# Sharing out the sum jobs of a gated decoder layer on one core, with the first scaling of u and the splitting of the next block's features moved

## What is computed

```python
h = rmsnorm(x, norm_mix_g)
z = gelu(h @ a_w_in)                        # 1024 -> 2048
u, v = split(z, 2)
v = rmsnorm(v, a_v_g)
ws = tril(a_w_s)                            # 8 groups of 128 x 128
s = einsum('gts,bnsgc->bntgc', ws, v) + a_b_s
x = x + (u * s) @ a_w_out
a = relu(rmsnorm(x, norm_mlp_g) @ mlp_w1)
x = x + (a * a) @ mlp_w2
out = rmsnorm(x, final_g)
```

## Time and profile before

| | |
|---|---|
| median of 3 runs | 1854.7 us |
| lowest, highest | 1849.44, 1864.49 us |
| the profiled execution | 1849.99 us |
| its span, first to last instruction | 1847.7 us |
| mean granted TensorE clock | 0.984 of full speed |
| PE busy | 1784.2 us (97%) |
| DVE busy | 1138.0 us (62%) |
| ACT busy | 786.1 us (43%) |
| POOL busy | 445.4 us (24%) |

### The profile page before, as it was taken

One profiled execution on the slowest core, in us unless ns is written; L12 is line 12 of the kernel. 1 busy time (PEld: TensorE's weight loads), 2 busy tenths in 40 slices (PEclk: granted clock), 3 DMA queues, 4 the chain that ended last, 5 costly groups with the idle time before them and its releaser, 6 DMA issues.

```text
span 1847.7 us, 20069 instructions
## 1 busy us (share of the span) xinstructions
PE 1784.2 (97%) x8036; PEld 1481.4 (80%) x8036; DVE 1138.0 (62%) x1136; ACT 786.1 (43%) x862; POOL 445.4 (24%) x418
## 2 busy tenths in 40 slices
PE   9999299999899999999999999999999999999998
PEld 8788188888688888888878888888888888888886
DVE  3561487456288665665576665676567666866665
ACT  5822325462423744443463434454433335333333
POOL 2443542443442123330001311110234101000002
PEclk9999599999999999999999999999999999999999
DMA  9556375765566788886867777699977645854552
GB/s 362 218 190 231 136 272 205 274 250 183 205 228 248 292 271 269 279 288 216 302 234 252 255 256 250 222 401 319 309 281 279 248 182 188 299 196 182 187 206 108
DMA packets 135452, 451.68 MB, mean 244 GB/s; under 512 B 8128, under 2 KB 9152, under 8 KB 119616
## 3 DMA queue, kind: packets, MB, share of 16 engines
q1 hardware_dynamic: 101344, 323.77, 49.5%
q0 software_dynamic: 27344, 101.19, 15.3%
q10 hardware_dynamic: 6672, 25.44, 3.7%
HBM read 320.35 MB, written 130.02 MB: 244 GB/s over the span
## 4 chain that ended last, share of the span: by engine, by line
PE 79%; DMA 10%; POOL 6%; ACT 3%; issue 2%; DVE 1%; ACTq 0%; DVEq 0%; POOLq 0%
PE bank L1448 64%; PE bank L1409 8%; PE bank L1260 4%; DMA job<-in_mlp_w 2%; DMA job<-xs 2%; DMA w1sum<-job 1%; PE bank L1249 1%; DMA job<-in_a_w_out 1%; DMA w_raw<-in_a_w_in 1%; ACT junk L653 1%; DMA wosum<-job 1%; DMA xs<-job 1%; POOL x_rstd L495 1%; PE bank L1282 1%; POOL job L529 1%
## 5 line engine op out<-in xcount | busy, mean ns | idle before, releaser
L1448 PE MATMUL bank<-x_hi,u_hi 128*128 128x512 f32 x896 | 349.1, 390 | 1.2 <-DVE c L1158 1.2
L1448 PE MATMUL bank<-x_hi,u_lo 128*128 128x512 f32 x896 | 348.6, 389 | 0.0
L1448 PE MATMUL bank<-x_lo,u_hi 128*128 128x512 f32 x896 | 348.6, 389 | 0.0
L1448 PE MATMUL bank<-d_lo,a_hi 128*128 128x512 f32 x896 | 348.5, 389 | 0.0
L1448 PE MATMUL bank<-d_hi,a_hi 128*128 128x512 f32 x896 | 348.5, 389 | 0.0
L1448 PE MATMUL bank<-d_hi,a_lo 128*128 128x512 f32 x896 | 348.5, 389 | 0.0
L1158 DVE TENSOR_TENSOR Y<-bank,Y 128x512 f32<-128x512 f32 x208 | 137.9, 685 | 179.1 <-PE bank L1448 178.7
L925 DVE TENSOR_TENSOR u_lo<-u_raw,u_hi 128x1024 fp32r<-128x1024 f32 x112 | 149.0, 1331 | 147.7 <-ACT u_hi L610 147.4
L615 ACT ACTIVATE d_hi<-d_raw 128x2048 fp32r<-128x2048 f32 x56 | 107.4, 1918 | 288.5 <-DMA d_raw<-w2sum 161.0
L919 DVE TENSOR_TENSOR w_lo<-w_raw,w_hi 128x2048 fp32r<-128x2048 f32 x45 | 108.2, 2411 | 150.3 <-ACT w_hi L605 150.3
L1448 PEld LDWEIGHTS bank<-x_hi,u_hi 128*128 128x128 f32 x896 | 168.2, 188 | 36.5 <-DVE u_lo L925 1.9
(11 more groups left out here) (125 smaller groups left out, 2791.9 us busy)
## 6 DMA issues: line engine op xcount, KB each, us to landing
a_raw<-a2s SPq DMA_DIRECT2D x56, 1024.0 KB, 7.8
a2s<-sums SPq DMA_DIRECT2D x32, 1280.0 KB, 8.1
job<-in_mlp_w POOLq DMA_DIRECT2D x32, 1024.0 KB, 7.0
u_raw<-w1sum SPq DMA_DIRECT2D x64, 512.0 KB, 4.7
d_raw<-w2sum SPq DMA_DIRECT2D x32, 1024.0 KB, 4.9
w_raw<-in_a_w_in SPq DMA_DIRECT2D x31, 1024.0 KB, 5.9
u_raw<-in_mlp_w SPq DMA_DIRECT2D x48, 512.0 KB, 5.3
d_raw<-in_mlp_w SPq DMA_DIRECT2D x24, 1024.0 KB, 5.3
```

Source lines behind the costliest of these rows:

```text
L1448: ins = pe.matmul(bank_of(g, j)[:, :], stationary[x_part][:, k, j * P:(j + 1) * P], moving[y_part][:, k, :], start=i in (0, 1, 3) and k == ...
```

## The change

Three edits. (1) POOL: the jobs of the four blocks are 1 and 2, 1 and 6, 1 and 2, 1 and 7 (before and behind the block's `rstd` of v) in place of 1 and 5, then 2 and 4 three times; 21 are done in the first stage in place of 24, and 19 in place of 15 in the groups u. (2) DVE: `scale_u(q, 0)` stands ahead of the remainder of weight w+8. (3) DVE: the remainders of the next block's features are made in two halves, the first behind weight w+9 (before the gates 2 and 3), the second behind gates 4 and 5; with it PE waits for four tiles before unit w and for the other four before unit w+1. The tiles and the number of instructions stay the same on every engine.

```diff
             for q in range(BLOCKS):
-                next_jobs(2 if q else 1)
+                next_jobs(1)
                 rstd(v_sq, v_squares(q), v_ms, v_ms_done, v_rstd, v_rstd_done, q)
...
-                next_jobs(4 if q else 5)
+                next_jobs((2, 6, 2, 7)[q])
...
             for u in range(UP):
                 pool.wait_ge(products, step_done(u * STEPS))
                 if not UP // PAIRS - 2 <= u <= UP // PAIRS:
-                    next_jobs(2 if u < 2 else 1)
+                    next_jobs(2 if u in (0, 1, 2, 3, 10, 12) else 1)
...
                 split_w(w + 7)
+                scale_u(q, 0)
                 split_w(w + 8)
-                scale_u(q, 0)
                 gates(q, 0)
                 split_w(w + 9)
                 if q % 2:
                     split_o(q // 2, 0)
+                else:
+                    split_h(q + 1, range(KU))
                 gates(q, 2)
-                if q % 2 == 0:
-                    split_h(q + 1, range(KD))
                 scale_u(q, 1)
                 gates(q, 4)
                 if q % 2 == 0:
+                    split_h(q + 1, range(KU, KD))
                     gates(q, 6)
...
                 if q:
-                    pe.wait_ge(hT_ready, q * KD + KD)
+                    pe.wait_ge(hT_ready, q * KD + KU)
...
                 token_major(hT[q], w, bank_set(q, 0), 0, first_v)
+                if q:
+                    pe.wait_ge(hT_ready, q * KD + KD)
                 token_major(hT[q], w + 1, bank_set(q, 0), 1, first_v_end)
```

## The result

The changed kernel takes 1835.03 us (median of 4 runs, 1834.01 to 1836.65) against 1855.33 us of the kernel before: ratio 0.9895, 95% interval 0.9859 to 0.9932. It is faster, by about 20 us or 1%, where 48 us were forecast. The profiled execution takes 1834.04 us with a span of 1831.7. This is outside the stated range of 1790 to 1825.

What follows compares the result with a forecast made beforehand. PE-bound, idling mainly 47.1 us in two waits for scale_u, held by v's rstd behind POOL's jobs. 1850.0 - 58.9 + 12.5 + 2 = 1805.6 us, 1810.3 by the median, stated as 1807; range 1790 to 1825.

Steps and rivals of the forecast that it cites:

- edit 1's first part: Blocks 1 and 3: fewer POOL jobs ahead of v's rstd, gain 47.1 us of PE waits and 5.4 of clock.
- rival (b): Blocks 1 and 3: the stall only shrinks, ACT or DVE late by 10 us in each; 1831 us, chance 0.07.
- Edits 2 and 3: First stage: PE's gaps of 1.65, 1.90 and 1.30 us go, with 1.5 of clock; gains 1.65 and 4.7 us.
- Rival (d): Edits 2 and 3 do nothing, the gaps having other causes: 1812 us; chance 0.70 together with the forecast.
- The 1.5 us of clock in the sum: Gain from the lowered clock at 108 to 116 us, behind PE's gap of 1.90 us, counted under edit 3.
- Edit 1's second part, the seven jobs: Block 3: seven POOL jobs behind v's rstd delay x1's rstd, late by 12.5 us plus 2 of clock.
- 2 x 15.9 + 4 x 18.6 + 11 = 117.2: Block 3's seven jobs undisturbed: two w1 jobs, four x jobs and the last; in time by 10 us against 126.8.
- 20.2 and 2 us: Added to the seven jobs: 20.2 for two slow ones in the projection, 2 for job 20's load beside five tiles.
- 2 of 12.8 us: Job 20's load beside five 1 MB tiles that take 12.8 us: it loses between 0 and all, taken as 2.
- 12.5 + 2: PE's new wait for x1 behind block 3, 12.5 us late plus 2 of clock; bounds 0 to 31.8.
- (a): Block 3's seven jobs are in time because they miss the loads: 1791 us, chance 0.20.
- (c): Block 3's seven jobs all take 29.3 us, late by 73 and 3 of clock: slower, 1867 us, chance 0.03.

Runs made afterwards that it cites:

- the short additions: The changed kernel with the additions of jobs 14 to 20 cut to one column of 512, most sums not computed: 1800.59 us, ratio 0.9724.
- the four-job version without edits 2 and 3: Kernel before with the operand's jobs at places 13 to 16, counts (2, 5, 2, 4) behind v's rstd: 1796.61 us, ratio 0.9687.
- edit 1 alone: The kernel before with only the jobs' counts changed, edits 2 and 3 left out: 1841.23 us, ratio 0.9936.

## Why the prediction was wrong

**What bounds the kernel, and edit 1's first part: right.** The rstd stood behind jobs; the waits of 36.97 and 10.17 us are gone in every run that does fewer jobs ahead of v's rstd. In the changed kernel POOL waits 7.49 and 34.46 us for squares instead, and no wait of the mixing for scale_u came in their place, so rival (b) is out. (The clock behind the first wait cost 0.4 us more than the 2.0 of the prediction, which left out 225 to 229 us, at 0.91.)

**Edits 2 and 3: right in size, with a condition that the prediction did not state.** About 6 us were measured where 1.65 + 4.7 were forecast, but only where the waits for POOL are gone. On top of the kernel before they gave nothing. Rival (d), which has them do nothing because the gaps had other causes, is out: the gaps go with the edits in every trace. The 1.5 us of clock in the sum are not sure: behind the same gap, of 1.57 to 2.18 us in three traces, the clock fell to 0.50 in two and not at all in the third, the one with the longest gap.

**Edit 1's second part, the seven jobs: right place, wrong size.** The step that failed is "2 x 15.9 + 4 x 18.6 + 11 = 117.2", with 20.2 and 2 us added. The chain took 160.3 us, not 139.4. I had taken two jobs of the trace, of 15.9 and 18.6 us, as the usual ones and put nearly all slowness in two others; the shortest of the seven takes 20.7 us. Taken apart by the same rows that the prediction used, its 139.4 us are some 44 of loads, 58 of additions and 37 of stores. Measured are 67.1, 54.2 and 39.0. So the additions took less than forecast and the loads 23 us more, which is more than the whole miss.

The reference jobs had loads of 5.2 and 6.1 us; from 531 us on, in the second half of the projection and at the handover, the three loads took 11.7, 9.2 and 17.8. The trace of before had no job to show this, since POOL idles there from 578 us on, but it had the traffic: the DMA engines are busy for 0.69 of the time from 578 to 590 us and 0.68 from 590 to 604, before any job is added. Its DMA issues also give longer medians than the quick jobs, 7.0 us from issue to landing for a job's load from the MLP weights and 8.1 from xs. For the last load I had taken 2 of 12.8 us; it was over 12 us longer than a quick one. The reason that I gave for it, five tiles at once, is at best a part: with the tiles issued in pairs the load was as long. Which of the transfers slows it stays open.

The wait came to 32.74 + 2.7 us in place of 12.5 + 2, and even the upper end of that term, 31.8, was below it.

**A term that was missing: the six jobs of block 1.** I checked them only against v's rstd and never set them against x1's, though `next_jobs` and two `rstd` stand behind block 1 just as behind block 3. It had four jobs behind it before and now six, 133.7 us of them (156.73 to 290.47). It cost 6.57 + 1.9 us, and moving one job away gave 9.3 us back. In the other traces with the same jobs up to there the gap is between 6.57 and 10.69 us, so its size is that of one execution.

Together: 20.9 us of the seven jobs' size (with the clock) and 8.5 of the missing term are 29.4; 1805.6 + 29.4 = 1835.0. The other rivals were no better in their mechanism: (a) had the seven jobs in time, and (c), slower with every job at 29.3 us, had the right mechanism with 7 x 29.3 where 160.3 was measured; the sign would have changed at 186.

## What to carry to other kernels

When work is moved behind a due point on an in-order queue, list every small step behind it on that queue, in each repetition of the loop, and give each a latest start; here two of four blocks had one, and one was looked at. Price the moved work for the part of the trace to which it goes: by the mean of its kind there, or, where it has no sample there, by what the DMA engines already carry. Price loads, work and stores apart; here the loads alone were wrong, 67 us for 44. The quickest sample is one that met little traffic. And a gain upstream of a wait counts only when that wait is paid off: the same two edits gave nothing before the counts were changed and about 6 us after.

## What was not expected of the hardware

An addition of one column (128 x 1) on POOL took 5.64 us against 0.19 for its neighbours, through four DVE instructions in a row. In this row it is not the size of POOL's work that sets its time beside a dense DVE stretch, but the end of DVE's run of instructions with two SBUF inputs; the row at 520.01 shows that such a run ends with a DVE instruction that reads PSUM as well as with a pause.

A load of 1 MB that keeps POOL idle for 4.4 us in the quiet stretches, and for 4.5 to 10.9 us in the first six of the seven jobs, kept it idle for 16.4 to 17.3 us at the handover between the stages, in five kernels with different jobs and different orders of the tiles there (and for 14.3 us with the short additions). The kernel before has one such load too, 20.86 us before the addition at 1332 us, where it costs PE nothing. That it is the sum of the traffic (DMA engines busy for 0.89 of the time from 572 to 605 us in the changed kernel) is likely; which of the transfers does it was not tried.

The length of a short idle gap of PE does not say what it costs in clock. At the same place of the program a gap of 1.57 us was followed by a granted clock of 0.50 (the four-job version without edits 2 and 3, 108 to 111 us), one of 1.90 us by 0.50 as well (the kernel before, 110 to 112 us), and one of 2.18 us by 1.00 (edit 1 alone, 109 to 117 us).
